# Summing squares for a norm: GpSimd adds and one product with ones, in place of eight ones-products

## The reference, cut to what matters

```
def rmsnorm(x, g):
    y = xf * lax.rsqrt(jnp.mean(xf * xf, axis=-1, keepdims=True) + EPS)
    return (y * g).astype(x.dtype)

for l in range(DEPTH):                       # DEPTH = 2
    h = rmsnorm(x, norm_g[l, 0]) * (1 + scale0) + shift0
    x = x + 0.5 * gate0 * rmsnorm(swiglu(h), norm_g[l, 1])
    h = rmsnorm(x, norm_g[l, 2]) * (1 + scale1) + shift1
    x = x + gate1 * rmsnorm(token_mixing(h), norm_g[l, 3])
    h = rmsnorm(x, norm_g[l, 4]) * (1 + scale2) + shift2
    x = x + 0.5 * gate2 * rmsnorm(swiglu(h), norm_g[l, 5])
```

## Time and profile before

| what | value |
|---|---|
| time, median of 3 runs | 2360.13 us (2358.76 to 2362.39) |
| the profiled execution's own time | 2360.49 us |
| its span in the profile | 2358.7 us |
| TensorE busy | 2328.1 us (99%) |
| VectorE busy | 1214.8 us (52%) |
| ScalarE busy | 564.3 us (24%) |
| GpSimd busy | 68.8 us (3%) |
| TensorE's mean granted clock | 0.999 |

### The profile page before, as it was taken

One profiled execution on the slowest core, in us unless ns is written; L12 is line 12 of the kernel. 1 busy time (PEld: TensorE's weight loads), 2 busy tenths in 40 slices (PEclk: granted clock), 3 DMA queues, 4 the chain that ended last, 5 costly groups with the idle time before them and its releaser, 6 DMA issues.

```text
span 2358.7 us, 41920 instructions
## 1 busy us (share of the span) xinstructions
PE 2328.1 (99%) x17408; PEld 2068.3 (88%) x17408; DVE 1214.8 (52%) x2557; ACT 564.3 (24%) x1349; POOL 68.8 (3%) x112
## 2 busy tenths in 40 slices
PE   7999999999999999999999999999999999999998
PEld 5999997886688699999999999977867886999998
DVE  4666422634756436665265663325355653566742
ACT  3000022114564231001130010311245642400011
POOL 0000000000022000000000000000000220000000
PEclk9999999999999999999999999999999999999999
DMA  9454234783389353443435533447715984233332
GB/s 333 159 179 155 98 126 148 233 269 101 124 298 337 124 193 108 143 144 99 134 136 179 180 127 99 165 148 227 249 68 184 329 290 147 73 108 108 99 121 77
DMA packets 300511, 390.15 MB, mean 165 GB/s; under 512 B 31005, under 2 KB 251033, under 8 KB 300322
## 3 DMA queue, kind: packets, MB, share of 16 engines
q1 hardware_dynamic: 281090, 336.41, 42.3%
q0 software_dynamic: 11712, 42.18, 5.2%
q10 hardware_dynamic: 7520, 8.87, 1.0%
HBM read 375.30 MB, written 12.12 MB: 164 GB/s over the span
## 4 chain that ended last, share of the span: by engine, by line
PE 97%; DMA 1%; SPq 1%; ACT 1%; issue 0%; DVE 0%; ACTq 0%; DVEq 0%
PE PS L734 31%; PE PS L834 13%; PE PS L1031 7%; PE PS L979 5%; PE PS L1298 4%; PE PS L925 4%; PE PS L674 3%; PE PS L1117 3%; PE PS L1197 3%; PE PS L1001 3%; PE PS L890 2%; PE PS L882 2%; PE PS L1338 2%; PE PS L1330 2%; PE PS L1237 2%; PE PS L1212 1%
## 5 line engine op out<-in xcount | busy, mean ns | idle before, releaser
L734 PE MATMUL PS<-OT,RING 128*128 128x192 f32 x1280 | 234.2, 326 | 0.0
L734 PE MATMUL PS<-H,RING 128*128 128x192 f32 x1280 | 222.1, 327 | 0.0
L734 PE MATMUL PS<-OT,QR 128*128 128x192 f32 x1280 | 221.1, 326 | 0.0
L734 PEld LDWEIGHTS PS<-OT,RING 128*128 128x128 f32 x1280 | 212.4, 190 | 0.0
L734 PEld LDWEIGHTS PS<-H,RING 128*128 128x128 f32 x1280 | 208.4, 190 | 3.8 <-issue 3.2
L734 PEld LDWEIGHTS PS<-OT,QR 128*128 128x128 f32 x1280 | 210.2, 190 | 0.0
L1447 ACT ACTIVATE QR<-QR 128x384 f32<-128x384 f32 x80 | 41.8, 523 | 532.9 <-DVE QR L2027 532.9
L1031 PE MATMUL PS<-H,RING 128*128 128x384 f32 x480 | 161.1, 490 | 0.0
L1031 PEld LDWEIGHTS PS<-H,RING 128*128 128x128 f32 x480 | 88.9, 190 | 60.6 <-issue 4.4
L734 PE MATMUL PS<-H,QR 128*128 128x192 f32 x640 | 117.1, 326 | 0.0
L734 PEld LDWEIGHTS PS<-H,QR 128*128 128x128 f32 x640 | 106.2, 190 | 0.0
(11 more groups left out here) (328 smaller groups left out, 4026.8 us busy)
## 6 DMA issues: line engine op xcount, KB each, us to landing
RING<-ffn_w_in SPq DMA_DIRECT2D x80, 1024.0 KB, 7.2
RING<-w_in SPq DMA_DIRECT2D x64, 768.0 KB, 6.3
QR<-w_ada SPq DMA_DIRECT2D x34, 1024.0 KB, 9.8
BIG<-w_ada SPq DMA_DIRECT2D x34, 1024.0 KB, 10.4
RING<-ffn_w_out SPq DMA_DIRECT2D x32, 768.0 KB, 4.6
RING<-ffn_w_out SPq DMA_DIRECT2D x32, 640.0 KB, 5.3
QR<-cache_sb_v POOLq DMA_DIRECT2D x16, 768.0 KB, 5.2
QKT<-cache_sb_k SPq DMA_DIRECT2D x16, 768.0 KB, 5.5
```

Of the source, the lines that this page charges most:

```text
L734: mm = pe.matmul(PS[:, bank, GROUP[g]], a[:, k, :], x[:, k, :], start=(k == 0), stop=(k == 3))
```

## The change

The eight products, the copy and the product with 1/32 of each pair of norm and group give way to seven adds on GpSimd, which gather the eight squares in tile 0 of `SQ`, each waiting for the square that it adds and for the add before it, and one product with a full 128 by 128 matrix of ones. The product waits until all seven adds are done. The places of the remaining products in TensorE's program are set anew. VectorE's copies go, and its `weight_sums` for the first prepared pair of a SwiGLU moves from the middle of the boundary (behind the sums of norm 2b+2) to behind the norm.

```
-        ONES = sb("ONES", 32)
-        MEAN = sb("MEAN", P)
+        ONES = sb("ONES", P)
...
-            def sums(q, g):
-                for k in range(KD):
-                    j = k % 4
-                    pe.wait_ge(sq_ready[g], 8 * q + k + 1)
-                    mm = pe.matmul(PS[32 * j:32 * j + 32, 6 + g, 0:HALF], ONES[:, :], SQ[:, k, GROUP[g]], start=(k < 4), stop=(k >= 4))
-                mm.then_inc(sums_ready[g], 1)
             def mean(q, g):
-                pe.wait_ge(sums_copied[g], q + 1)
-                pe.matmul(PS[:, 6 + g, 0:HALF], MEAN[:, :], VAR[:, GROUP[g]], start=True, stop=True).then_inc(ms_ready[g], 1)
+                pe.wait_ge(sq_added[g], 7 * q + 7)
+                pe.matmul(PS[:, 6 + g, 0:HALF], ONES[:, :], SQ[:, 0, GROUP[g]], start=True, stop=True).then_inc(ms_ready[g], 1)
...          # swiglu_in, first products of group 0 (before line 755)
                             if b >= 0 and p == 0 and part == 0 and k == 3:
-                                sums(2 * b + 1, 1)
-                            if b >= 0 and p == 0 and part == 0 and k == 6:
                                 mean(2 * b + 1, 1)
-                            if b >= 0 and p == 1 and part == 1 and k == 1:
-                                sums(2 * b + 2, 1)
-                            if b >= 0 and p == 1 and part == 1 and k == 4:
+                            if b >= 0 and p == 1 and part == 1 and k == 7:
                                 mean(2 * b + 2, 1)
...          # swiglu_out, last products of group 1 (before line 892)
-                            if half == 0 and m == 0 and k == 4:
-                                sums(2 * b + 1, 0)
-                            if half == 0 and m == 0 and k == 7:
+                            if half == 0 and m == 0 and k == 3:
                                 mean(2 * b + 1, 0)
-                            if half == 1 and m == 0 and k == 4 and b < 5:
-                                sums(2 * b + 2, 0)
-                            if half == 1 and m == 0 and k == 7 and b < 5:
+                            if half == 1 and m == 0 and k == 9 and b < 5:
                                 mean(2 * b + 2, 0)
...
+            def add_squares(q, g, ks):
+                for k in ks:
+                    if k:
+                        pool.wait_ge(sq_ready[g], 8 * q + k + 1)
+                        if k > 1:
+                            pool.wait_ge(sq_added[g], 7 * q + k - 1)
+                        nc.gpsimd.tensor_tensor(SQ[:, 0, GROUP[g]], SQ[:, 0, GROUP[g]], SQ[:, k, GROUP[g]], ALU.add).then_inc(sq_added[g], 1)
+            def ffn_squares(b):
+                for m in range(2 * SEVEN_OUT):
+                    for g in range(2):
+                        add_squares(2 * b + 1, g, (m,))
+                add_squares(2 * b + 1, 0, (6, 7))
+                if b < 5:
+                    add_squares(2 * b + 2, 0, range(KD))
+                add_squares(2 * b + 1, 1, (6, 7))
+                if b < 5:
+                    add_squares(2 * b + 2, 1, range(KD))
+            for g in range(2):
+                add_squares(0, g, range(KD))
...          # DVE, boundary(b)
                     scale_x(b + 1)
-                    sums(2 * b + 2, 1)
-                    if b % 3:
-                        weight_sums((b + 1) // 3, (b + 1) % 3 // 2, PLAIN)
                     pre_norm(b + 1, 1)
```

42 lines of the change are left out of this document (15 added, 27 removed).

## The result

The changed kernel takes 2370.16 us (median of 6 runs, 2366.26 to 2373.35), the kernel before, on the same chip, 2360.31 (2358.76 to 2362.39). The ratio is 1.0038, with a 95% interval of 1.0028 to 1.0048: slower by 9.9 us, where 2351.9 and "faster" were predicted, and above the end of the range (2366). The profiled execution is the slowest of the six: 2373.35 us, with a span of 2371.6, against 2358.7 before.

What follows compares the result with a forecast made beforehand. TensorE, busy 99% of the span with 97% of the chain of waits, was taken as the bound. 2360.5 - 20.4 - 0.9 + 5.2 + 3.0 + 0.5 + 4.0 = 2351.9 us, range 2343 to 2366.

Steps and rivals of the forecast that it cites:

- The gain per pair: TensorE's sums of one norm and group: removing them gains 0.97 us, for 21 pairs in dense work 20.4 us.
- The price of an add: GpSimd's add of 192 columns: 0.6 us each, consecutive adds 0.70 us apart, range 0.4 to 0.95.
- The start: Norm 0: fourteen adds delay the second mean, VectorE goes on at 27.9 instead of 22.68; 5.2 us lost.
- Norm 2b+1, group 1: Boundaries behind a SwiGLU (0, 2, 3): TensorE waits 1.0 us for the last add, three times; 3.0 us lost.
- The other eight: Remaining means of norm 2b+1, group 0 and the mixer's boundaries: nearly no wait, 0.5 us lost for all eight.
- Norm 2b+2: Adds beside VectorE's work at a sublayer's end: free without sharing, up to 16.4 us with it; 4 us lost taken.
- The upper bound: Norm 2b+2 if every VectorE and GpSimd instruction holds up the other: 16.4 us lost over three groups 0, five groups 1.
- The rule of the Trainium skill: VectorE with two SBUF inputs and GpSimd reading SBUF: the first to start blocks the other fully; 16.4 us, not 4.
- The tail: Last pair, norm 11 group 1, a bare chain: 1.77 us from square to mean becomes about 0.8; 0.9 us gained.
- Moved work: `weight_sums` behind the norm makes the sums over tokens about 1 us later, GpSimd's loads unaffected; costs nothing.
- B: Rival: VectorE and GpSimd block each other fully; 2364.3 us by upper bound, 2360 expected, no measurable change; chance 0.18.
- C: Rival: slower because an add is slow, 1.0 us between adds; 2369 us; chance 0.17.

Runs made afterwards that it cites:

- e6: Changed kernel with the ten pairs of norm 2b+2 summed by products again, at the earlier kernel's places; 2358.27 us, ratio 0.9989 to the kernel before.
- e3: Changed kernel with the second operand of VectorE's 16 operations read from PSUM, computation altered (x gets the factor); 2350.18 us, ratio 0.9952 to the kernel before.
- e14: Changed kernel with one more VectorE wait, a gap of about 0.12 us ahead of the train's sixth operation; 2355.74 us, ratio 0.9972 to the kernel before.
- e11: Lone kernel, none of the reference computed: 140 VectorE trains differing in the moment GpSimd's first add is requested; no first add longer than 0.83 us.
- e13: Lone kernel: 37 VectorE trains, GpSimd's add requested at different operations; gets in up to 1.43 us into the train, held from 1.65 us on.
- e5: Lone kernel: seven VectorE trains, GpSimd's first of seven chained adds released by ScalarE; first adds last 0.62 to 0.80 us.
- e9: Lone kernel: five short VectorE trains, varying waits, ScalarE's squares and TensorE; first adds 0.74 us (stages 1, 4), 0.63 (3), 2.66 (2, 5).
- e7: Changed kernel with GpSimd adds for norms 2b+1 alone and group 1's mean four products later in the SwiGLU; 2354.80 us, ratio 0.9976 to the kernel before.
- e16: e14 with norm 0 summed by products, means at the changed kernel's places; 2351.87 us, ratio 0.9962 to the kernel before.
- e15: e14 with norm 0 summed by products and group 1's means of norm 2b+1 four products later; 2357.34 us, ratio 0.9982 to the kernel before.

## Why the prediction was wrong, step by step

- **The gain per pair** (0.97 us forecast): 0.93 in the ledger. Right.
- **The price of an add** (0.6 us, 0.70 apart): 0.59 and 0.71. Right, though the way to it, the ratio of two memsets of one column, was no evidence about an add of 192: that it hit is partly luck. The estimate of 0.42 us before dispatch from the Trainium skill (GPSIMD Engine Reference, section 3.1) is 0.17 us below what these traces show for the whole add. By it the adds would be 0.52 apart, 2.5 us less at the start alone.
- **The start** (5.2): 5.95 in the ledger: 5.55 until VectorE goes on (28.23 against 22.68), the rest since the 64 products at 27.20 ran at half clock (3.64 us instead of 1.96), which was in no term; in whole runs 2.8 to 4.0.
- **Norm 2b+1, group 1** (1.0 us three times, 3.0): 1.7 three times, 5.1. The place was right and the size was off, because the squares were taken at their old time. The change also puts the second mean of group 0 later, by 28 products; ScalarE's scaling of h follows that mean, and now ends in front of squares 6 and 7:
```profile
357.05 3.16 ACT L1381 ACTIVATE H<-H,MOD 128x192 f32<-128x192 f32 x7
360.12 0.30 ACT L1390 ACTIVATE OT<-PS 128x192 f32<-128x192 f32 x1
```
  Less the shift of 5.95, square 6 comes at 354.17 instead of 353.44, 0.73 us later. In e6, where the second norm stands as before, the steps at these places are +0.06 net, a loss of 0.99 (0.78 idle), as forecast. The other eight (0.5) cost nothing.
- **Norm 2b+2** (4.0): 21.5 us, of which 5.3 are half clock. This is the step that failed, and it carries the sign: with 4.0 there the ledger's sum is -3.3 us, some 2357. The sum took a value near the lower end, "because TensorE, ScalarE and VectorE read SBUF together throughout this trace and VectorE's add keeps its 0.351 us mean". That was evidence about other engines, and VectorE's mean did stay at 0.35: it is not VectorE that is held. The upper bound of 16.4 us was met in its mechanism (2.93 us of hold, and the scale of x holding one more: e3, e6 and e14 show it) and without the clock also in its size (16.2). It was exceeded by the clock, which fell behind three of these waits (2.1 to 2.4 us) and was in no term.
- **The rule of the Trainium skill** (SBUF — State Buffer, section "Who interferes with whom"), weighed against the sum at this place, was the better guide. The runs agree that two SBUF inputs on VectorE are what matters (e3: 20 us less with one of them in PSUM). That the one that starts first blocks the other holds for the first add only in part: beside one VectorE instruction it waits at most 0.24 us (e11), beside a train from the seventh operation on it waits for all of it (e13).
- **The tail** (0.9 gained): 1.2 lost. The last mean did come 1.05 us nearer to its square, but ScalarE was then copying an output tile, and turned to it 1.72 us behind the mean's start (2357.92), where it was 0.67 before, so nothing was left of it; some 1.2 us more are lost behind that norm, by a cause that no run tested. After, and then before:
```profile
2358.49 0.60 ACT L1765 ACTIVATE QR<-PS 128x512 f32<-128x512 f32 x1 [0.43 <-ACT QR L1765]
...
2359.64 0.42 ACT L1371 ACTIVATE NORM<-PS,EPSC 128x192 f32<-128x192 f32 x1 [0.56 <-ACT QR L1765]
```
```profile
2347.97 0.42 ACT L1399 ACTIVATE NORM<-PS,EPSC 128x192 f32<-128x192 f32 x1 [0.56 <-PE PS L668]
```
- **Moved work** (0): no wait of TensorE on it shows. Right.
- **The rivals.** B named the mechanism, with 2364.3 us by the upper bound; its "2360 at the middle, since some adds can run in VectorE's gaps" was wrong, since a train of operations 0.27 us apart and 0.35 long has none. C came nearest in number, 2369, by luck: its adds 1.0 us apart are not there (0.71).

## What to carry to other kernels

Before work is given to GpSimd beside a VectorE stretch with two SBUF operands, count at which of VectorE's back-to-back operations the request falls: with operations of 192 columns, a request early in the train cost VectorE 0.4 us per instruction here, and one from the seventh operation on cost GpSimd the rest of the train. A single wait that opens a gap in the train was worth 14.4 us here, and an operand in PSUM 20, beside the 19.5 that the removed products gave. And when a wait before a fixed chain of other engines is taken away, look for it behind the chain before counting it as saved.

## What was not expected of the hardware

- An add of GpSimd (128x192, two SBUF operands) asked for during the first six of VectorE's back-to-back operations got in within 0.24 us, in all 156 lone trains so released (e5, e11, e13); asked for from the seventh on it was held until the train ended (1.05 to 2.92 us, 24 trains of e13 and two of e9). Waits in VectorE's operations that open no gap, ScalarE, TensorE, the phase and who wrote the data do not matter; a gap does (e9, e14).
- The kernels' own traces put the border inside the sixth operation. At boundaries 1 and 4 VectorE works five operations of 192 columns behind GpSimd's last turn and then narrower ones of 128, 0.20 us apart. Asked for 1.45 us behind the start of the first of the five, during the sixth operation, the add got in (e6 and e7, four records of 0.62 us); asked for at 1.49 to 1.52 us, during the sixth too, it was held until the end of the train (e14 to e16, six records of 1.56 to 1.60 us). Boundary 1 in e6 and in e14:
```profile
870.25 0.62 POOL L1821 TENSOR_TENSOR OT<-OT 128x192 f32<-128x192 f32 x1 [1.59 <-ACT OT L1420]
```
```profile
870.78 1.58 POOL L1790 TENSOR_TENSOR OT<-OT 128x192 f32<-128x192 f32 x1 [1.65 <-ACT OT L1390]
```
  Whether VectorE's time since the last gap or turn decides, or the number of its operations, is open.
- Once in, chained adds and VectorE take turns: VectorE's operation beside each add takes 0.74 us instead of 0.35, and the add 0.59, or 0.79 where it is asked for just behind one of VectorE's (e14).
- With the second operand in PSUM neither waits (8.55 us of train and 0.59 per add), and VectorE's pitch stays 0.27 us even when it writes to PSUM as well.
- In dense work, idle stretches of TensorE of 1.9 to 2.4 us at the second mean were followed by half clock in part of the cases: in the changed kernel behind 2.10 (twice) and 2.41 us and not behind 2.09 and 2.12, 1.7 to 1.9 us more each, and in e15 behind two of five waits of 1.9 us. At the first mean, with 1.5 us idle, the granted clock stayed full.
